# Two scale chunks of the first condition as column products, a freed bank for the first shift, a separate semaphore for one load, and wide products in the last norm

## The chip, the cores and the metric

The kernel runs on one core of a Trainium2 chip. The time is the device time of one execution in microseconds. Five engines work side by side: TensorE (PE; its weight loads are listed as PEld), VectorE (DVE), ScalarE (ACT), GpSimd (POOL) and SyncE (SP), which issues all the DMAs. They meet only at semaphores.

## The reference

Input `x` (256 tokens of 1024 features) and a context `ctx` of 256 tokens pass through two transformer layers with adaptive norms, then `x` alone through a hybrid layer and a last norm. What the change touches is the very first norm and the very last:

```python
def adaln(cond, w, b):
    m = jax.nn.silu(cond) @ w + b
    return m.reshape(m.shape[:-1] + (N_MOD, D_MODEL))

def modulated_norm(h, g, m, k):
    return rmsnorm(h, g) * (1.0 + m[..., k + 1, :]) + m[..., k, :]
...
m = adaln(c, ada_w[i], ada_b[i])[:, None]
mc = adaln(c_ctx, ada_w[i], ada_b[i])[None]
h = half_ffn(h, m, 0, g[0], g[1], ffn_w_in[i, 0], ffn_w_out[i, 0])
...
return rmsnorm_2(x, norm_final)
```

There are two conditions, `c` for the latents and `c_ctx` for the context. `m[k]` is called the shift and `m[k+1]` the scale. `ada_w` has 9 x 1024 columns for each of the two layers, and all are needed, but the first norm needs only the first 1024 (shift) and the next 1024 (scale) of layer 0.

## The kernel before

Activations are kept transposed: features on the 128 partitions, in 8 chunks `c` (`CH` is 8), and tokens along the free axis, 512 of them (context and latents) in the first two layers and 256 at the end. Every product with a weight is made as three fp32r products, `w_hi·u_hi`, `w_lo·u_hi`, `w_hi·u_lo` (lines 1555, 1556, 1559). ScalarE rounds each raw weight tile to `w_hi` (line 771), GpSimd subtracts to get `w_lo` (line 751), in a ring of six tiles. The activations are split alike into `u_hi` (ACT, line 837) and `u_lo` (DVE, line 1186). The order of work on each engine is the order in which the code is written.

**The opening.** The norm's total over features is one product with ones (line 1684); ACT makes `rstd` of it (lines 791 and 799), signalled as `first_rstd`. For each chunk `c`:

- The shift's 128 values for both conditions are made on TensorE by `shift(c)`: eight products of a 128x128 piece of `ada_shift[c]` with the 2-column `silu_t` (line 1693), into bank `SUMS + c % 2`. ACT adds the bias (line 854, tile `mcol`).
- The scale's 128 values are made on DVE by two dot products over 1024 elements, one for each condition (`dot`, line 1104, tile `ada_sum`, with `silu_c`, the silu of the condition spread over all partitions, line 843). `a_col` (line 1268) is `(scale + 1) * gain`.
- DVE then makes `v = h * a_col * rstd` for both token halves (line 1172), and between them `u_lo` of the chunk before (line 1186). ACT makes `u_hi` of `v` and the shift.
- TensorE multiplies chunk `k` of `u` with four weight tiles, twelve 512-column products, after it has made `shift(k + 1)`: for `k` of 2 and more the order on TensorE is `shift(k + 1)`, then the twelve products of chunk `k`. The last of each three waits for `u_lo` of its chunk.

After chunk 7, DVE starts the first feed-forward block: 18 steps `m`, in each of which it makes two more tiles of `ada_w` (four dots) and then the gate product of step `m` (lines 1321, 1324, 1326). TensorE may start step `m` when the gate of step `m - 3` is there.

**The end.** In the last feed-forward block, the residual is added chunk by chunk as TensorE finishes it (DVE, line 1336), ACT squares it (line 814) and DVE sums the squares (line 1167). Two products with ones and two ACT instructions give `rstd`, and DVE makes the output in eight products of 256 columns, `h * gain * rstd` (line 1538). SyncE stores it in three DMAs (line 738), chunks 0 to 2, 3 to 5, 6 and 7.

Of the kernel before, what the change touches and what calls it, by code (L numbers as in the profile page):

```python
# [28 lines left out]
RAW_ITEMS = 9  # L29
FULL_U = slice(0, 256)  # L30
# [12 lines left out]
ADA_FREE = 4  # L43
ADA_OUT = (3, 3, 3, 3, 2, 2)
# [309 lines left out]
def build(nc, A):  # L354
# [110 lines left out]
    scale_in, shift_in = [sem(f"scale_in{c}") for c in range(CH)], [sem(f"shift_in{c}") for c in range(CH)]  # L465
    first_sq, first_sum, first_rstd = sem("first_sq"), sem("first_sum"), sem("first_rstd")
# [12 lines left out]
    out_ready, out_done = sem("out_ready"), sem("out_done")  # L479
# [44 lines left out]
    def norm_gain(b, m, c):  # L524

        if m is None:
            g = COL["norm2"] + b["part"] * CH + c
            return col[:, g:g + 1]
        return a_col[:, 3 * m + b["part"], c:c + 1]

# [136 lines left out]
    def _(sp):  # L667
# [68 lines left out]
        for c0, c1 in ((0, 3), (3, 6), (6, CH)):  # L736
            sp.wait_ge(out_ready, c1)
            sp.dma_start(A["out"][:, c0:c1, :], final[:, c0:c1, :]).then_inc(out_done, 16)
# [24 lines left out]
    def _(act):  # L763
# [76 lines left out]
        def first_norm(b):  # L840
            heads_to(0)
            act.wait_ge(consts_in, 32)
# [8 lines left out]
            for c in range(CH):  # L851
                act.wait_ge(shift_sum, c + 1)
                bias = COL["ada_b"] + c
                scalar.activation(mcol[:, :, c:c + 1], psum[:, SUMS + c % 2, 0:2].rearrange("p (c o) -> p c o", o=1),
# [71 lines left out]
        def output(b):  # L926
# [23 lines left out]
            for i, (j, tok, _) in enumerate(pieces):  # L950
# [127 lines left out]
    def _(dve):  # L1078
# [15 lines left out]
        dve.wait_ge(consts_in, 32)  # L1094
# [161 lines left out]
        def first_norm(b):  # L1256
# [6 lines left out]
            for c in range(CH):  # L1263
                dve.wait_ge(scale_in[c], 16)
                for i in range(2):
                    dot(first_tile(c), i, 2 * c + i, 0, ada_sum[:, c % 2, i:i + 1], 0)
                dve.wait_ge(ada_dot, 2 * c + 2 + ADA0)
                vec.tensor_scalar(a_col[:, 0:6:3, c:c + 1], ada_sum[:, c % 2, :].rearrange("p (c o) -> p c o", o=1),
# [9 lines left out]
            for p, tok in enumerate(halves(FULL)):  # L1278
                u_low(b, p, tok, CH - 1)
            dve.sem_inc(m_done, ADA_FIRST)  # L1280
# [255 lines left out]
        for c in range(CH):  # L1536
            g = COL["norm2"] + 3 * CH + c
# [5 lines left out]
    def _(pe):  # L1543
# [136 lines left out]
        def start_phase(b, tiles):  # L1680
# [32 lines left out]
            for k in range(2, CH):  # L1713
                if k + 1 < CH:
                    shift(k + 1)
# [362 lines left out]
```

## Time and profile before

| | |
|---|---|
| median of 3 runs | 2410.27 us (2409.76 to 2411.99) |
| profiled execution, its own time | 2406.9 us |
| its span | 2405.0 us |
| PE busy | 2329.1 us (97%) |
| DVE busy | 1577.9 us (66%) |
| ACT busy | 910.3 us (38%) |
| POOL busy | 1354.8 us (56%) |
| opening, up to DVE's first dot of the feed-forward block | 61.66 us |
| granted clock, mean | 0.999 |

The span is the time from the first to the last recorded instruction or transfer; the execution's own time is 1.9 us longer. The profiled execution was 3.4 us shorter than the median of the timed ones. A row of the timeline gives the start, the duration, the engine, the line and the operation with the tile it writes and the ones it reads; in brackets stands how long the engine had been idle and what it had waited for. "x16" is a count of merged instructions. A plain fp32 product is recorded as two instructions, so the eight products of one shift are a row of x16.

### The profile page before, as it was taken

How to read it: one execution, taken by the hardware profiler on the slowest of the kernel's cores; microseconds unless marked ns; L12 is line 12 of the kernel's file. 1: busy time of each engine (PE TensorE's matmuls, PEld its weight loads, DVE VectorE, ACT ScalarE, POOL GpSimd, SP SyncE). 2: the span in 40 equal slices, each digit the busy share in tenths (PEclk: the TensorE clock that was granted, in tenths of full speed). 3: DMA queues.
4: the chain of work that ended last, by engine and by line, in shares of the span. 5: the costliest groups of instructions: out<-in, count | busy, mean ns of one | idle time of the engine just before them, and what ended most of it. 6: DMA issues, size and time to landing. Idle time of an engine off the chain costs nothing.

```text
span 2405.0 us, 36289 instructions
## 1 busy us (share of the span) xinstructions
PE 2329.1 (97%) x14528; PEld 2062.9 (86%) x14528; DVE 1577.9 (66%) x2518; ACT 910.3 (38%) x1466; POOL 1354.8 (56%) x700
## 2 busy tenths in 40 slices
PE   7999999999989999999999998899999999999998
PEld 5887789777688777898778897789999999999998
DVE  8999796666679997958983126567527614534661
ACT  4222224455442222233222235554444444545443
POOL 4555455222235554654554443278878887468886
PEclk9999999999999999999999999999999999999999
DMA  7655352211025553534533332145555564345554
GB/s 278 214 189 184 139 206 85 71 54 62 27 88 202 196 182 139 205 109 166 178 129 93 97 90 72 53 149 184 179 156 192 180 189 159 99 145 185 183 179 136
DMA packets 97510, 350.11 MB, mean 146 GB/s; under 512 B 10944, under 2 KB 10944, under 8 KB 96960
## 3 DMA queue, kind: packets, MB, share of 16 engines
q1 hardware_dynamic: 97344, 347.81, 43.2%
q8 instruction: 115, 1.88, 0.3%
q14 instruction: 51, 0.42, 0.1%
HBM read 346.71 MB, written 1.05 MB: 145 GB/s over the span
## 4 chain that ended last, share of the span: by engine, by line
PE 51%; DVE 13%; issue 4%; ACT 2%; POOL 1%; DMA 1%; DVEq 0%; ACTq 0%
PE psum L1555 16%; PE psum L1559 16%; PE psum L1556 16%; DVE psum L1104 7%; PE psum L1904 1%; DVE sq L1321 1%; POOL w_lo L751 1%; PE psum L1876 1%; ACT w_hi L771 1%; DVE gu_hi L1324 0%; DVE psum L1194 0%; DVE h L1200 0%; PE psum L1884 0%; DVE u_lo L1413 0%; DVE pcomb L1386 0%
## 5 line engine op out<-in xcount | busy, mean ns | idle before, releaser
L751 POOL TENSOR_TENSOR w_lo<-w_raw,w_hi 128x1024 fp32r<-128x1024 f32 (+3 forms) x696 | 1354.6, 1971 | 1033.4 <-ACT w_hi L771 1032.7
L1555 PE MATMUL psum<-u_hi,w_hi 128*128 128x256 f32 (+2 forms) x2912 | 975.4, 335 | 16.3 <-POOL w_lo L751 5.3
L1559 PE MATMUL psum<-u_lo,w_hi 128*128 128x256 f32 (+2 forms) x2912 | 947.8, 325 | 3.3 <-DVE u_lo L1186 2.0
L1556 PE MATMUL psum<-u_hi,w_lo 128*128 128x256 f32 (+2 forms) x2912 | 945.8, 325 | 0.0
L771 ACT ACTIVATE w_hi<-w_raw 128x1024 fp32r<-128x1024 f32 (+1 forms) x522 | 529.1, 1030 | 337.7 <-PE psum L1559 275.5
L1555 PEld LDWEIGHTS psum<-u_hi,w_hi 128*128 128x128 f32 x2912 | 553.1, 190 | 98.2 <-issue 25.7
L1559 PEld LDWEIGHTS psum<-u_lo,w_hi 128*128 128x128 f32 x2912 | 552.7, 190 | 52.8 <-DVE u_lo L1186 4.8
L1556 PEld LDWEIGHTS psum<-u_hi,w_lo 128*128 128x128 f32 x2912 | 553.4, 190 | 44.3 <-issue 3.4
L1555 PE MATMUL psum<-gu_hi,w_hi 128*128 128x256 f32 (+1 forms) x1188 | 379.2, 319 | 0.0
L1556 PE MATMUL psum<-gu_hi,w_lo 128*128 128x256 f32 (+1 forms) x1188 | 378.1, 318 | 0.0
L1559 PE MATMUL psum<-gu_lo,w_hi 128*128 128x256 f32 (+1 forms) x1188 | 378.1, 318 | 0.0
L1555 PEld LDWEIGHTS psum<-gu_hi,w_hi 128*128 128x128 f32 x1188 | 226.3, 190 | 15.8
L1556 PEld LDWEIGHTS psum<-gu_hi,w_lo 128*128 128x128 f32 x1188 | 226.3, 191 | 15.7
L1559 PEld LDWEIGHTS psum<-gu_lo,w_hi 128*128 128x128 f32 x1188 | 226.3, 190 | 15.3
L918 ACT ACTIVATE sq<-psum 128x512 f32<-128x512 f32 x66 | 39.5, 599 | 456.1 <-DVE gu_lo L1326 399.5
L1326 DVE TENSOR_TENSOR gu_lo<-sq,gu_hi 128x512 fp32r<-128x512 f32 (+1 forms) x132 | 184.3, 1396 | 4.5
L1104 DVE CUSTOM_DVE_ANT_0 psum<-ada_lo,silu_c 128x1024 f32<-128x1024 f32 x96 | 170.1, 1772 | 10.1 <-DMA ada_lo<-in_ada_w 8.5
L1210 DVE TENSOR_TENSOR rstd<-rstd,sq 128x256 f32<-128x256 f32 (+1 forms) x58 | 43.1, 743 | 192.0 <-ACT sq L867 99.6
L1104 DVE CUSTOM_DVE_ANT_0 psum<-ada_hi,silu_c 128x1024 f32<-128x1024 f32 x96 | 160.1, 1668 | 1.7
L1124 DVE TENSOR_SCALAR mcol<-ada_sum,col 128x2 f32<-128x2 f32 x128 | 151.0, 1180 | 4.5
L1321 DVE TENSOR_TENSOR sq<-sq,psum 128x512 f32<-128x512 f32 (+1 forms) x110 | 63.6, 578 | 78.6 <-PE psum L1559 71.6
L1324 DVE CAST gu_hi<-sq 128x512 fp32r<-128x512 f32 (+1 forms) x132 | 102.9, 780 | 4.6
(173 smaller groups left out, 2060.4 us busy)
## 6 DMA issues: line engine op xcount, KB each, us to landing
w_raw<-in_ffn_in SPq DMA_DIRECT2D x264, 512.0 KB, 3.7
w_raw<-in_ffn_out SPq DMA_DIRECT2D x96, 448.0 KB, 3.4
ada_hi<-in_ada_w SPq DMA_DIRECT2D x48, 512.0 KB, 3.6
ada_lo<-in_ada_w SPq DMA_DIRECT2D x48, 512.0 KB, 3.5
w_raw<-in_ffn_out SPq DMA_DIRECT2D x48, 512.0 KB, 3.6
ada_out<-in_ada_w SPq DMA_DIRECT2D x32, 512.0 KB, 4.4
w_raw<-in_b_qkv SPq DMA_DIRECT2D x30, 512.0 KB, 3.4
w_raw<-in_da_in SPq DMA_DIRECT2D x24, 512.0 KB, 3.5
```

Source lines behind the costliest of these rows:

```text
L751: last = pool.tensor_tensor(w_lo[:, slot, w], w_raw[:, slot, w], w_hi[:, slot, w].bitcast(F32), ALU.subtract)
L771: scalar.activation(w_hi[:, slot, 0:cols], w_raw[:, slot, 0:cols], ACT.Copy).then_inc(hi_ready, 1)
L918: scalar.activation(s_up[:, j, tok], psum[:, pair_bank(m), tok], ACT.Silu).then_inc(silu_ready, 1)
L1104: vec.tensor_tensor_reduce(out=psum[:, junk:junk + 2, :].rearrange("p a b -> p (a b)"), in0=tile, in1=silu_c[:, c, :], scale=1.0, scalar=0 ...
L1124: vec.tensor_scalar(mcol[:, :, n:n + 1], ada_sum[:, n % 2, :].rearrange("p (c o) -> p c o", o=1), col[:, bias:bias + 1], None, ALU.add).th ...
L1210: vec.tensor_tensor(sqsum[:, tok], sqsum[:, tok], sq[:, i % 2, tok], ALU.add).then_inc(yacc_ready, 1)
L1321: vec.tensor_tensor(s_up[:, j, tok], s_up[:, j, tok], psum[:, pair_bank(m) + 1, tok], ALU.mult)\
L1324: vec.tensor_copy(gu_hi[:, m, tok], s_up[:, j, tok]).then_inc(ghi_ready, 1)
L1326: vec.tensor_tensor(gu_lo[:, m, tok], s_up[:, j, tok], gu_hi[:, m, tok].bitcast(F32), ALU.subtract)\
L1555: mm(out, w_hi[:, slot, w], x_hi, start=start and n == 0, stop=False)
L1556: mm(out, w_lo[:, slot, w], x_hi, start=False, stop=False)
L1559: last = mm(out, w_hi[:, slot, w], x_lo, start=False, stop=stop and n == len(ks) - 1)
```

## The change

Four edits.

1. `SCALE_COLS = 2`: the scale of chunks 6 and 7 is no longer made by dots on DVE. Its weights come in the layout of the shift's (`ada_scale`), and TensorE makes it with eight 2-column products per chunk, in `scale(c)`, into bank 0 or 1. `scale(6)` stands after `shift(6)` and ahead of the products of chunk 5, `scale(7)` after `shift(7)` and ahead of the products of chunk 6. DVE waits for the sum (`scale_sum`) before it makes `a_col`.
2. The first shift goes into bank `RSTD` instead of `SUMS`, which holds the norm's total; so `shift(0)` no longer waits for `first_rstd`, and `shift(1)` does.
3. The load of `silu_c` has a semaphore of its own, so that its silu waits for that load and not for the table of columns too; ACT waits for the columns before it adds the first shift's bias.
4. In the last norm ACT makes `h * gain` of each chunk after its square, and DVE multiplies with `rstd` in three products of 768, 768 and 512 columns instead of eight of 256.

```diff
-        sp.dma_start(silu_c[:, :, :], A["cond"]).then_inc(consts_in, 16)
+        sp.dma_start(silu_c[:, :, :], A["cond"]).then_inc(silu_c_in, 16)
         for c in range(CH):
-            sp.dma_start(first_tile(c), A["ada_w"][CH + c]).then_inc(scale_in[c], 16)
+            by_cols = c >= CH - SCALE_COLS
+            scale = A["ada_scale"][c - CH + SCALE_COLS] if by_cols else A["ada_w"][CH + c]
+            sp.dma_start(first_tile(c), scale).then_inc(scale_in[c], 16)
...
-            act.wait_ge(consts_in, 32)
+            act.wait_ge(silu_c_in, 16)
             scalar.activation(silu_c[:, :, :], silu_c[:, :, :], ACT.Silu).then_inc(silu_c_ready, 1)
...
                 act.wait_ge(shift_sum, c + 1)
+                if c == 0:
+                    act.wait_ge(consts_in, 16)
...
                     square(nb, 0, LAT, j)
+                    if nb["n"] == len(BLOCKS):
+                        g = COL["norm2"] + 3 * CH + j
+                        scalar.activation(final[:, j, :], h[:, j, LAT], ACT.Copy, scale=col[:, g:g + 1]).then_inc(final_gain, 1)
...
             for c in range(CH):
-                dve.wait_ge(scale_in[c], 16)
-                for i in range(2):
-                    dot(first_tile(c), i, 2 * c + i, 0, ada_sum[:, c % 2, i:i + 1], 0)
-                dve.wait_ge(ada_dot, 2 * c + 2 + ADA0)
+                if c < CH - SCALE_COLS:
+                    dve.wait_ge(scale_in[c], 16)
+                    for i in range(2):
+                        dot(first_tile(c), i, 2 * c + i, 0, ada_sum[:, c % 2, i:i + 1], 0)
+                    dve.wait_ge(ada_dot, 2 * c + 2 + ADA0)
+                    total = ada_sum[:, c % 2, :]
+                else:
+                    dve.wait_ge(scale_sum, c - CH + SCALE_COLS + 1)
+                    total = psum[:, c % 2, 0:2]
...
-        for c in range(CH):
-            g = COL["norm2"] + 3 * CH + c
-            vec.scalar_tensor_tensor(out=final[:, c, :], in0=h[:, c, LAT], scalar=col[:, g:g + 1], in1=psum[:, RSTD, LAT],
-                                     op0=ALU.mult, op1=ALU.mult).then_inc(out_ready, 1)
+        for n, c in enumerate(FINAL_PARTS):
+            dve.wait_ge(final_gain, c.stop)
+            k = c.stop - c.start
+            vec.tensor_tensor(final[:, c, :], final[:, c, :], psum[:, RSTD:RSTD + 1, LAT].broadcast_to([128, k, SEQ]), ALU.mult)\
+               .then_inc(out_ready, 1)
...
             def shift(c):
                 pe.wait_ge(shift_in[c], 16)
-                if c == 0:
+                if c == 1:
                     pe.wait_ge(first_rstd, 1)
...
+            def scale(c):
+
+                pe.wait_ge(scale_in[c], 16)
+                if c == CH - SCALE_COLS:
+                    pe.wait_ge(ada_dot, 2 * c + ADA0)
+                for k in range(CH):
+                    last = mm(psum[:, c % 2, 0:2], first_tile(c)[:, k * 128:(k + 1) * 128], silu_t[:, k, :],
+                              start=k == 0, stop=k == CH - 1)
+                last.then_inc(scale_sum, 1)
...
                 if k + 1 < CH:
                     shift(k + 1)
+                if k >= CH - 1 - SCALE_COLS and k + 1 < CH:
+                    scale(k + 1)
                 for tile in tiles:
                     run(*tile, k)
```

TensorE in the opening, from the last products of chunk 4 on, before: `shift(6)` stands between them and the products of chunk 5 (`first_b` holds the shift's weights).

```order
L1559 MATMUL psum<-u_lo,w_hi 128x512 [waits ulo_ready]
L1693 MATMUL psum<-silu_t,first_b 128x2 [waits shift_ready,shift_in6]
L1693 MATMUL psum<-silu_t,first_b 128x2 x7
L1555 MATMUL psum<-u_hi,w_hi 128x512 [waits uhi_ready]
L1556 MATMUL psum<-u_hi,w_lo 128x512
L1559 MATMUL psum<-u_lo,w_hi 128x512 [waits ulo_ready]
```

The same place after the change; the row with `first_a` is `scale(6)`.

```order
L1580 MATMUL psum<-u_lo,w_hi 128x512 [waits ulo_ready]
L1714 MATMUL psum<-silu_t,first_b 128x2 [waits shift_ready,shift_in6]
L1714 MATMUL psum<-silu_t,first_b 128x2 x7
L1724 MATMUL psum<-silu_t,first_a 128x2 [waits ada_dot,scale_in6]
L1724 MATMUL psum<-silu_t,first_a 128x2 x7
L1576 MATMUL psum<-u_hi,w_hi 128x512 [waits uhi_ready]
L1577 MATMUL psum<-u_hi,w_lo 128x512
L1580 MATMUL psum<-u_lo,w_hi 128x512 [waits ulo_ready]
```

Eight more 2-column products stand ahead of chunk 5's, and in the same way ahead of chunk 6's; nothing else on TensorE has moved.

VectorE in the opening, chunk 6, before (`v_63` is the tile `v` of the text; ISA is a dot or the reading of its sum):

```order
L1104 ISA psum,ada_sum<-first_a,silu_c 128x1024 [waits ada_dot,scale_in6]
L1104 ISA ada_sum 128x1
L1104 ISA psum,ada_sum<-first_a,silu_c 128x1024 [waits ada_dot]
L1104 ISA ada_sum 128x1
L1268 TENSOR_SCALAR a_col<-ada_sum,stat,col 128x2 [waits ada_dot]
L1172 SCALAR_TENSOR_TENSOR v_63<-h,a_col,rstd 128x256 [waits scale_step]
L1186 SCALAR_TENSOR_TENSOR u_lo<-v_63,mcol,u_hi 128x256 [waits uhi_ready]
L1172 SCALAR_TENSOR_TENSOR v_63<-h,a_col,rstd 128x256
L1186 SCALAR_TENSOR_TENSOR u_lo<-v_63,mcol,u_hi 128x256 [waits uhi_ready]
```

The same chunk after:

```order
L1287 TENSOR_SCALAR a_col<-psum,stat,col 128x2 [waits scale_sum]
L1186 SCALAR_TENSOR_TENSOR v_63<-h,a_col,rstd 128x256 [waits scale_step]
L1200 SCALAR_TENSOR_TENSOR u_lo<-v_63,mcol,u_hi 128x256 [waits uhi_ready]
L1186 SCALAR_TENSOR_TENSOR v_63<-h,a_col,rstd 128x256
L1200 SCALAR_TENSOR_TENSOR u_lo<-v_63,mcol,u_hi 128x256 [waits uhi_ready]
```

The two dots are gone from chunk 6 and from chunk 7. The `u_lo` in these rows is that of the chunk before, so `u_lo` of chunk 5 still stands behind `a_col` of chunk 6, which now waits for TensorE.

VectorE at the end, before:

```order
L1336 SCALAR_TENSOR_TENSOR h<-psum,h 128x256 [waits tile_used]
L1167 TENSOR_TENSOR sq<-psum,sq 128x256 [waits hacc_ready,hsq_ready]
L1538 SCALAR_TENSOR_TENSOR final<-h,col,psum 128x256 [waits hsq_ready,hacc_ready,rstd_h_ready]
L1538 SCALAR_TENSOR_TENSOR final<-h,col,psum 128x256 x7
L1977 UNCONDITIONAL_BRANCH
```

And after:

```order
L1356 SCALAR_TENSOR_TENSOR h<-psum,h 128x256 [waits tile_used]
L1181 TENSOR_TENSOR sq<-psum,sq 128x256 [waits hacc_ready,hsq_ready]
L1559 TENSOR_TENSOR final<-final,psum 128x768 [waits hsq_ready,hacc_ready,final_gain,rstd_h_ready]
L1559 TENSOR_TENSOR final<-final,psum 128x768 [waits final_gain]
L1559 TENSOR_TENSOR final<-final,psum 128x512 [waits final_gain]
L2010 UNCONDITIONAL_BRANCH
```

Eight instructions have become three, and eight copies with a gain have been added on ScalarE, one behind each square.

## Rows read from the trace of the kernel before

**Rows 1.** The page: span, and shares of the last chain by engine.
```profile
span 2405.0 us, 36289 instructions
...
PE 51%; DVE 13%; issue 4%; ACT 2%; POOL 1%; DMA 1%; DVEq 0%; ACTq 0%
```
**Rows 2.** Windows: stretch, length, busy us (instructions) by engine, clock, DMA, GB/s.
```profile
50.80:55.32 4.52, 4.52 (x29) 3.96 (x28) 4.42 (x10) 0.91 (x3) 0.00 (x0) 1.00 0.00 0
...
61.60:264.40 202.80, 201.83 (x880) 164.22 (x879) 199.08 (x238) 46.66 (x56) 113.76 (x36) 1.00 0.54 189
```
**Rows 3.** Waits from 63 to 270 us: total us, times, longest.
```profile
PEld psum L1555 <- DVE sq L1321: 5.5, 9, 1.3
```
**Rows 4.** Timeline of DVE, chunks 5 to 7 and the first body dot.
```profile
50.28 0.48 DVE L1186 SCALAR_TENSOR_TENSOR u_lo<-v,mcol,u_hi 128x256 fp32r<-128x256 f32 x1
50.68 1.23 DVE L1104 CUSTOM_DVE_ANT_0 psum<-first_a,silu_c 128x1024 f32<-128x1024 f32 x1
...
53.33 0.29 DVE L1268 TENSOR_SCALAR a_col<-ada_sum,stat,col 128x2 f32<-128x2 f32 x1
...
54.84 0.48 DVE L1186 SCALAR_TENSOR_TENSOR u_lo<-v,mcol,u_hi 128x256 fp32r<-128x256 f32 x1
...
60.52 0.89 DVE L1186 SCALAR_TENSOR_TENSOR u_lo<-v,mcol,u_hi 128x256 fp32r<-128x256 f32 x2 [0.64 <-ACT u_hi L837]
...
61.66 1.23 DVE L1104 CUSTOM_DVE_ANT_0 psum<-ada_hi,silu_c 128x1024 f32<-128x1024 f32 x1
```
**Rows 5.** Timeline of PE, products of chunk 4, `shift(6)`, chunk 5, `shift(7)`.
```profile
50.82 0.50 PE L1559 MATMUL psum<-u_lo,w_hi 128*128 128x512 f32 x1
...
53.24 1.84 PE L1693 MATMUL psum<-silu_t,first_b 128*128 128x2 f32 x16
...
54.94 0.49 PE L1555 MATMUL psum<-u_hi,w_hi 128*128 128x512 f32 x1
...
57.80 1.84 PE L1693 MATMUL psum<-silu_t,first_b 128*128 128x2 f32 x16
```
**Rows 6.** Timeline of ACT: the bias of shift 6.
```profile
55.11 0.26 ACT L854 ACTIVATE mcol<-psum,col 128x2 f32<-128x2 f32 x1 [3.61 <-PE psum L1693]
```
**Rows 7.** Timeline of the opening's start: ACT, DVE, PE.
```profile
13.65 1.91 ACT L843 ACTIVATE silu_c<-silu_c 128x2048 f32<-128x2048 f32 x1 [1.40 <-DMA col<-in_columns]
...
15.69 1.23 DVE L1104 CUSTOM_DVE_ANT_0 psum<-first_a,silu_c 128x1024 f32<-128x1024 f32 x1 [0.51 <-ACT silu_c L843]
...
18.37 6.96 PE L1693 MATMUL psum<-silu_t,first_b 128*128 128x2 f32 x32 [2.85 <-ACT rstd L799]
...
27.10 0.80 PE L1559 MATMUL psum<-u_lo,w_hi 128*128 128x512 f32 x1 [0.70 <-DVE u_lo L1186]
```
**Rows 8.** Timeline of SP and DVE: a tile for the body's third ada step.
```profile
64.25 0.91 SPq L677 DMA_DIRECT2D ada_lo<-in_ada_w  x2
...
73.25 1.22 DVE L1104 CUSTOM_DVE_ANT_0 psum<-ada_lo,silu_c 128x1024 f32<-128x1024 f32 x1
```
**Rows 9.** Timeline of PE: 512-column products early and later, and a long wait.
```profile
28.54 0.63 PE L1559 MATMUL psum<-u_lo,w_hi 128*128 128x512 f32 x1
...
41.55 0.40 PE L1559 MATMUL psum<-u_lo,w_hi 128*128 128x512 f32 x1
...
427.03 1.22 PE L1589 MATMUL psum<-sq,ones 128*128 128x256 f32 x2 [2.65 <-DVE sq L1167]
```
**Rows 10.** Timeline of the end, and a 512-column DVE product on PSUM.
```profile
82.78 0.68 DVE L1321 TENSOR_TENSOR sq<-sq,psum 128x512 f32<-128x512 f32 x1
...
2396.01 0.41 DVE L1167 TENSOR_TENSOR sq<-psum,sq 128x256 f32<-128x256 f32 x1
...
2397.65 0.47 ACT L791 ACTIVATE rstd<-psum,small 128x256 f32<-128x256 f32 x1 [0.94 <-PE psum L1594]
...
2398.57 3.22 DVE L1538 SCALAR_TENSOR_TENSOR final<-h,col,psum 128x256 f32<-128x256 f32 x8 [2.15 <-ACT psum L799]
...
2399.86 2.29 SPq L738 DMA_DIRECT2D out<-final  x3
```

More of the change, by code:

```diff
@@ L29 @@
 RAW_ITEMS = 9
+FINAL_PARTS = (slice(0, 3), slice(3, 6), slice(6, CH))
 FULL_U = slice(0, 256)
@@ L43 @@
 ADA_FREE = 4
+SCALE_COLS = 2
 ADA_OUT = (3, 3, 3, 3, 2, 2)
@@ L529, in norm_gain, with shift_bank @@
         return a_col[:, 3 * m + b["part"], c:c + 1]
+    def shift_bank(c):
+        return (RSTD, SUMS)[c % 2]
     def gate_bank(j):
@@ L735, in _ @@
                 load_whole(A[b["kind"] + "_out"], b["t_out"], 0, CH)
-        for c0, c1 in ((0, 3), (3, 6), (6, CH)):
-            sp.wait_ge(out_ready, c1)
-            sp.dma_start(A["out"][:, c0:c1, :], final[:, c0:c1, :]).then_inc(out_done, 16)
+        for n, c in enumerate(FINAL_PARTS):
+            sp.wait_ge(out_ready, n + 1)
+            sp.dma_start(A["out"][:, c, :], final[:, c, :]).then_inc(out_done, 16)
         sp.wait_ge(out_done, 48)
@@ L1279, in first_norm @@
                 u_low(b, p, tok, CH - 1)
+            dve.sem_inc(ada_dot, 2 * SCALE_COLS)
             dve.sem_inc(m_done, ADA_FIRST)
@@ L1534, in _ @@
             transition(b, BLOCKS[b["n"] + 1] if b["n"] + 1 < len(BLOCKS) else END)
-        for c in range(CH):
-            g = COL["norm2"] + 3 * CH + c
-            vec.scalar_tensor_tensor(out=final[:, c, :], in0=h[:, c, LAT], scalar=col[:, g:g + 1], in1=psum[:, RSTD, LAT],
-                                     op0=ALU.mult, op1=ALU.mult).then_inc(out_ready, 1)
+        for n, c in enumerate(FINAL_PARTS):
+            dve.wait_ge(final_gain, c.stop)
+            k = c.stop - c.start
+            vec.tensor_tensor(final[:, c, :], final[:, c, :], psum[:, RSTD:RSTD + 1, LAT].broadcast_to([128, k, SEQ]), ALU.mult)\
+               .then_inc(out_ready, 1)
     @block.tensor
@@ L1692, in shift @@
                 for k in range(CH):
-                    last = mm(psum[:, SUMS + c % 2, 0:2], first_tile(CH + c)[:, k * 128:(k + 1) * 128], silu_t[:, k, :],
+                    last = mm(psum[:, shift_bank(c), 0:2], first_tile(CH + c)[:, k * 128:(k + 1) * 128], silu_t[:, k, :],
                               start=k == 0, stop=k == CH - 1)
                 last.then_inc(shift_sum, 1)
+            def scale(c):
[6 more added lines that the diff above has]
+                last.then_inc(scale_sum, 1)
             def run(t, bank, tok, k):
@@ L2048 @@
     X["ada_shift"] = I["ada_w"][0][:, 0:D].reshape(CH, 128, CH, 128).transpose(2, 1, 0, 3).reshape(CH, 128, D)
+    n = 2 * D - SCALE_COLS * 128
+    X["ada_scale"] = I["ada_w"][0][:, n:2 * D].reshape(CH, 128, SCALE_COLS, 128).transpose(2, 1, 0, 3).reshape(SCALE_COLS, 128, D)
     X["ada_w"] = I["ada_w"].reshape(2, D, MODS, 128).transpose(0, 2, 3, 1).reshape(2 * MODS, 128, D)
```

9 lines of the change are left out of this document (5 added, 4 removed).

## The prediction, made before the changed kernel was run

> **What bounds the kernel now.** I read the page first: the chain that ended last lies 51% on TensorE and 13% on VectorE [rows 1]. Then the windows, to see where VectorE's part lies. From 61.6 to 264.4 us, the steps of the first feed-forward block that also make `ada_w` tiles, VectorE is busy 199.08 of 202.80 us [rows 2], and the little that is missing lies between single instructions; TensorE waits there for VectorE's gate products, 9 times and 5.5 us in all counted on its weight loads [rows 3]. So that stretch ends when VectorE is through, and it starts when VectorE leaves the opening, at 61.66 us [rows 4]. After it TensorE is the bound up to the end of the kernel but for the last norm. Whatever moves VectorE's 61.66 us moves the end by as much, as long as TensorE can follow.
>
> Last I read the opening itself, instruction by instruction. From chunk 4 on, the two engines go in step. TensorE waits for `u_lo` of chunk 4, which VectorE ends at 50.76 us (50.28 + 0.48) [rows 4], and goes on at 50.82 [rows 5]. In the window from 50.80 to 55.32 both are full: TensorE 4.52 and VectorE 4.42 of 4.52 us [rows 2]. The same work of the next chunk starts 4.56 us later on TensorE (53.24 and 57.80), so a chunk costs each of them about 4.56 us, side by side [rows 5].
>
> **The change, part by part.** All times below are those of the profiled execution: 2406.9 us, 1.9 more than its span.
>
> *Scale 6 and 7 on TensorE.* VectorE loses two dots per chunk, 53.33 - 50.68 = 2.65 us each time [rows 4]. TensorE gains a second block of eight 2-column products, at 1.84 us as `shift(6)` and `shift(7)` show it; I take 1.85 [rows 5]. By busy time alone this looks like a good trade, 5.3 us off VectorE for 3.7 on TensorE. What decides is the order. `u_lo` of chunk 5 stands on VectorE behind `a_col` of chunk 6, which now waits for `scale(6)`, and `scale(6)` stands on TensorE behind `shift(6)`, which stands behind all of chunk 4's products. And chunk 5's last factor on TensorE is that `u_lo`. What ran side by side becomes a row:
>
> - `shift(6)` has its result at 55.11, where ScalarE takes it [rows 6]. `scale(6)` has its result 1.85 later, at 56.96.
> - VectorE has been idle since 50.76 and now makes `a_col`, `v`, `u_lo`, `v`, `u_lo`. From the start of `a_col` to the end of the last `u_lo` it took 54.84 + 0.48 - 53.33 = 1.99 us [rows 4]. So `u_lo` of chunk 5 is whole at 58.95 instead of 55.32: 3.63 us later.
> - TensorE has passed `scale(6)` and two products of chunk 5 by then and stands still for some 1.3 us. Everything behind moves by 3.63 us: `shift(7)` too. The same happens once more with `scale(7)`: `u_lo` of chunk 6 is 7.26 us later.
> - `u_lo` of chunk 7 used to wait 0.64 us for ScalarE [rows 4], because shift 7 came late; it is now long there. So VectorE leaves the opening 7.26 - 0.64 = 6.6 us later.
>
> The end of VectorE's work is what the body hangs on, so this is +6.6 us at 264 us too. TensorE itself leaves the opening up to 7.3 us later; with up to 5.5 us of waits in the body to give back [rows 3] it would be late by 1.8 to 5 alone, so VectorE stays the bound. SyncE's next loads wait for TensorE to free a tile; the pair for the third ada tile was issued at 64.25 and used at 73.25 [rows 8]. The issue moves by 7.3 and the use by 6.6, so of 9 us between them 8.3 are left for a load that is half a megabyte as before. No new wait there.
>
> Bounds of the term: if the small block costs nothing beside what VectorE does, only the 1.99 us in a row stay for each chunk and the wait is smaller; by the rows the least is TensorE's own extra work, 2 x 1.85 = +3.7, less the short waits it has now, at most 0.7 as at 27.10 [rows 7]: +3. At most the term is 2 x (1.85 + 1.99 + 0.3) = +8.3, with an exchange of signals dearer than now. I take +6.6.
>
> *The load of silu_c.* ScalarE sat idle 1.40 us until the table of columns had landed, and VectorE then idle 0.51 us for the silu [rows 7]. VectorE cannot gain more than its own 0.51, since the instruction ahead of its first dot needs the columns. It is the bound from there, so I take -0.5; bounds 0 and -0.5.
>
> *The first shift in a free bank.* TensorE waited 2.85 us for `rstd` and no longer does [rows 7]. But it then waited 0.70 us for `u_lo` of chunk 0 at 27.10, which VectorE makes after the dots of chunk 1. The shift is earlier and the wait longer by the same amount. I take 0; bounds -0.7 (if ScalarE's earlier conversions get GpSimd out of VectorE's way sooner) and +0.5 (if they fall on it at a worse time).
>
> *The last norm.* Eight products took 3.22 us, 0.40 each [rows 10]. A product of 256 columns that reads PSUM took 0.41, one of 512 took 0.68 us [rows 10]: 0.27 for 256 columns more, so 0.95 for 768. Three of them are 0.95 + 0.95 + 0.68 = 2.58, less some 0.08 of overlap at each joint, 2.45. The gain is 0.75. The last store still follows the last product. ScalarE's copy of the last chunk lies in the 0.94 us in which it waits for TensorE [rows 10], if it is as long as its neighbours, 0.4 to 0.5; the seven others lie between tiles, where ScalarE has idle time. Bounds: -1.2, if width costs less than the rows say, and +0.5, if the repeated read of one bank is slow. I take -0.7.
>
> *Sum.* +6.6 - 0.5 + 0 - 0.7 = +5.4 us: 2406.9 becomes 2412.3 in a profiled execution. The median of the timed runs was 3.4 us above this one, so beside the median 2410.27 it is 2415.7 us.
>
> **A rule against this change.** At 28.54 us a 512-column product takes 0.63 us, at 41.55 it takes 0.40 [rows 9]: the first is the lower level, 1.2 GHz, and the second 2.4, though the granted clock stands at 1.00 in the windows. The 6.96 us of 2-column products from 18.37 on [rows 7] did not bring the clock up. A wait of 2.65 us between products of ones did not bring it down [rows 9]. The change puts blocks of 3.7 us of 2-column products and a wait of 1.3 us in a row, twice, with only ten full products between them. The trace has nothing like it at the upper level. If the clock fell there, the second pair of blocks and the products of chunks 6 and 7 would run at the lower one: 1.85 x 2 more for the small blocks, and about 3 more on TensorE behind them, of which VectorE sees only the first part: +3.7 on the sum, up to +5. The Trainium skill, "TensorE: Matmul & The Clock Gate", section "HAM oscillation — how this bites in real kernels", says that TensorE is set back to half rate when it stands idle too long between bursts. By that rule such a chunk order is at risk; by the row with 2.65 us it is not yet.
>
> **The rivals.**
>
> - *The clock falls* (12%): as above, +5.4 + 3.7 = +9.1, 2419.4 us. For: small products did not raise it. Against: none of the long waits in this kernel brought it down.
> - *VectorE catches up in the body* (20%): its dots there meet GpSimd's subtractions differently when TensorE and VectorE are shifted, and TensorE's own path decides. Then +7.3 - 5.5 - 0.5 - 0.7 = +0.6 at the least and some +3 in the middle: 2413 us, within the resolution. Against it: VectorE has no wait in 203 us.
> - *The trade works* (8%): `scale(6)` is there when VectorE arrives at it at 50.8. Then VectorE saves 5.3 and leaves at -5.8, TensorE has +3.7 - 0.5 = +3.2, less up to 5.5 given back [rows 3]; the later of the two decides: -2.3 at best, with the last norm -3.0, 2407.3 us. It decides only if `scale(6)` is through before 50.8, and in the written order it cannot start before the products of chunk 4 are. This one ends faster than before.
> - *My mechanism* (60%): 2413.5 to 2418 us, with the terms' bounds.
>
> **How the numbers follow.** A measurement of this kernel can tell 0.2% from no change, 4.8 us here: slower means above 2415.1, faster below 2405.5. My mechanism is centred 0.6 above the line, so about 60% of its 60 lie above it, 38 in 100; the fallen clock gives 12 and the catching up 2: 52 in 100 slower. Faster needs the trade to work and more than its price, or a term I have not seen: 6. The rest, 42, is no change to be told. The range 2409 to 2420.5 leaves out the trade that works, and the dearest case of the clock.
>
> **What would show it.** In the changed profile: VectorE idle some 6 us between the `u_lo` of chunk 4 and `a_col` of chunk 6, released by the small products on TensorE (`first_a`), and again some 6 before chunk 7; TensorE waiting 1.3 to 2 us for `u_lo` after the first two products of chunks 5 and 6; the first body dot at about 67.8 us instead of 61.66; VectorE as full in the body as before, and step 18 of the body later by the same 6; first dot of all at 15.2; `final` in three rows, 2.5 us in all. It is wrong if VectorE's first body dot comes before 64 us, or if the body gives back more than 1 us of its delay, or if 512-column products behind the small blocks take 0.63 us.

## The result: 0.5% slower, and the profile after

| | before | after |
|---|---|---|
| median | 2410.33 us (2407.70 to 2411.99, 6 runs) | 2422.04 us (2416.01 to 2422.37, 6 runs) |
| ratio | | 1.0045, 95% interval [1.0034, 1.0056] |
| profiled execution, its own time | 2406.9 us | 2422.03 us |
| its span | 2405.0 us | 2420.2 us |
| first dot of the feed-forward block | 61.66 us | 71.24 us |
| ScalarE's first `u_hi` of the second block | 407.24 us | 418.04 us |

The forecast was +5.4 us, 2415.7 (2409 to 2420.5). The sign was the likelier one, but +11.7 us lies outside the range.

VectorE in the opening of the changed kernel, to be set beside [rows 4]:

```profile
49.73 0.48 DVE L1200 SCALAR_TENSOR_TENSOR u_lo<-v,mcol,u_hi 128x256 fp32r<-128x256 f32 x1
57.92 0.28 DVE L1287 TENSOR_SCALAR a_col<-psum,stat,col 128x2 f32<-128x2 f32 x1 [7.71 <-PE psum L1724]
...
68.21 0.28 DVE L1287 TENSOR_SCALAR a_col<-psum,stat,col 128x2 f32<-128x2 f32 x1 [8.30 <-PE psum L1724]
...
71.24 1.23 DVE L1118 CUSTOM_DVE_ANT_0 psum<-ada_hi,silu_c 128x1024 f32<-128x1024 f32 x1
...
78.01 0.69 DVE L1346 TENSOR_TENSOR gu_lo<-sq,gu_hi 128x512 fp32r<-128x512 f32 x1
82.44 2.89 DVE L1118 CUSTOM_DVE_ANT_0 psum<-ada_lo,silu_c 128x1024 f32<-128x1024 f32 x1 [3.74 <-DMA ada_lo<-in_ada_w]
```

The two waits of `a_col` for the column sums (L1724) are those that were forecast, but 7.71 and 8.30 us long. At 82.44 stands one that was not: VectorE waits 3.74 us for a tile of `ada_w`.

TensorE at the same place, to be set beside [rows 5]; L1714 is the shift, L1724 the scale, and the row at 65.42 is `scale(7)`, whose weights lie in a tile named `first_b`:

```profile
45.71 0.69 PE L1580 MATMUL psum<-u_lo,w_hi 128*128 128x512 f32 x1 [0.79 <-DVE u_lo L1200]
46.20 0.63 PE L1576 MATMUL psum<-u_hi,w_hi 128*128 128x512 f32 x1
...
54.25 1.84 PE L1714 MATMUL psum<-silu_t,first_b 128*128 128x2 f32 x16
55.95 1.93 PE L1724 MATMUL psum<-silu_t,first_a 128*128 128x2 f32 x16
...
59.96 0.79 PE L1580 MATMUL psum<-u_lo,w_hi 128*128 128x512 f32 x1 [1.50 <-DVE u_lo L1200]
60.55 0.63 PE L1576 MATMUL psum<-u_hi,w_hi 128*128 128x512 f32 x1
...
65.42 2.74 PE L1724 MATMUL psum<-silu_t,first_b 128*128 128x2 f32 x16
68.03 0.77 PE L1576 MATMUL psum<-u_hi,w_hi 128*128 128x512 f32 x1
68.60 0.63 PE L1577 MATMUL psum<-u_hi,w_lo 128*128 128x512 f32 x1
70.25 0.80 PE L1580 MATMUL psum<-u_lo,w_hi 128*128 128x512 f32 x1 [1.02 <-DVE u_lo L1200]
```

A 512-column product is recorded with 0.39 us at the upper level (2.4 GHz) and 0.63 at the lower (1.2 GHz); the records of neighbours overlap, so that the next one starts 0.23 or 0.43 us later. The level fell three times: at 45.7, behind a shift and a wait of 0.79; at 60, behind `shift(6)`, `scale(6)` and a wait of 1.50; and in `scale(7)`, which takes 2.74 us where `scale(6)` took 1.93. The first of the three stands ahead of every product that the change adds. Windows of the same stretch (columns as in [rows 2]) show it as granted clock:

```profile
45.00:50.00 5.00, 4.29 (x14) 3.47 (x14) 4.89 (x10) 0.57 (x2) 0.37 (x1) 0.66 0.00 0
...
50.21:60.00 9.79, 8.29 (x59) 7.32 (x59) 1.95 (x5) 2.40 (x6) 0.00 (x0) 0.97 0.00 0
60.00:75.00 15.00, 13.98 (x59) 11.60 (x60) 6.65 (x15) 2.75 (x6) 0.00 (x0) 0.68 0.00 1
75.00:87.00 12.00, 12.00 (x55) 9.93 (x54) 8.05 (x13) 4.85 (x6) 5.66 (x3) 1.00 0.91 347
```

The loads of the body: SyncE issues `ada_lo` behind the last products of chunk 7, at 75.92 where it was 64.25 [rows 8], and they share the DMA engines with all the others (0.91 in the window above).

```profile
74.86 1.01 SPq L689 DMA_DIRECT2D w_raw<-in_ffn_in  x2
75.92 0.91 SPq L684 DMA_DIRECT2D ada_lo<-in_ada_w  x2
```

The opening's first rows, beside [rows 7], and the tail, beside [rows 10]:

```profile
12.68 1.91 ACT L852 ACTIVATE silu_c<-silu_c 128x2048 f32<-128x2048 f32 x1 [0.64 <-DMA silu_c<-in_cond]
...
14.99 1.23 DVE L1118 CUSTOM_DVE_ANT_0 psum<-first_a,silu_c 128x1024 f32<-128x1024 f32 x1
...
16.01 3.58 PE L1714 MATMUL psum<-silu_t,first_b 128*128 128x2 f32 x16 [0.69 <-DMA first_b<-in_ada_shift]
...
26.39 0.80 PE L1580 MATMUL psum<-u_lo,w_hi 128*128 128x512 f32 x1 [1.91 <-DVE u_lo L1200]
...
2412.33 0.49 ACT L974 ACTIVATE final<-h,col 128x256 f32<-128x256 f32 x1
...
2414.30 2.42 DVE L1559 TENSOR_TENSOR final<-final,psum 128x768 f32<-128x768 f32 x3 [2.15 <-ACT psum L808]
```

VectorE's first dot is 0.70 us earlier, the first shift no longer waits for `rstd` (its wait has gone to `u_lo`, 1.91 instead of 0.70), and the three wide products take 2.42 us instead of 3.22. In these rows the small edits do what they were meant to.

### The profile page after: what moved, and what is told of

Same layout as the page of the kernel before. It is cut to its first block, busy times and chain, and to the rows that moved or that the text cites. A ratio compares the mean times of both kernels' runs of the same rounds, so it can differ in the third digit from the quotient of the medians.

```text
span 2420.2 us, 36350 instructions
## 1 busy us (share of the span) xinstructions
PE 2342.9 (97%) x14560; PEld 2075.7 (86%) x14560; DVE 1567.3 (65%) x2505; ACT 913.7 (38%) x1474; POOL 1354.1 (56%) x700
## 4 chain that ended last, share of the span: by engine, by line
PE 44%; DVE 7%; issue 2%; ACT 2%; DMA 0%; POOL 0%; DVEq 0%; ACTq 0%
PE psum L1576 14%; PE psum L1580 14%; PE psum L1577 14%; DVE psum L1118 3%; PE psum L1937 1%; PE psum L1909 1%; ACT w_hi L780 1%; PE psum L1917 0%; POOL w_lo L760 0%; DVE u_lo L1433 0%; DVE sq L1341 0%; DVE pcomb L1406 0%; DVE stat L1491 0%; DVE psum L1208 0%; DMA w_raw<-in_ga_in 0%
```

## The experiments

Eleven kernels ran, each timed against the kernel before on the same chip. "First dot" is VectorE's first of the feed-forward block, "second block" ScalarE's first `u_hi` there, both in the profiled execution; the clock is the mean granted clock of all the runs, beside that of the kernel before on the same chip. Microseconds beside before are the ratio times 2410; the kernel before took 2411.50, 2410.45 and 2410.87 us in the median on the chips of the experiments, so two kernels are better compared by their ratios than by their medians.

Theory A, when the first runs were made: the order makes a row (TensorE's small products, VectorE's wait, TensorE's wait), and that is the price. B: the early first shift disturbs the clock's rise. C: TensorE's extra small products and their clock are the price.

| kernel | median us | ratio, 95% | first dot | second block | clock (before) |
|---|---|---|---|---|---|
| before | 2410.33 | | 61.66 | 407.24 | |
| after | 2422.04 | 1.0045 [1.0034, 1.0056] | 71.24 | 418.04 | 0.9938 |
| e1, small edits alone | 2409.53 | 0.9996 [0.9988, 1.0005] | 61.27 | 406.74 | 0.9963 (0.9962) |
| e10, same, early loads | 2410.50 | 0.9993 [0.9985, 1.0002] | 61.30 | 406.90 | 0.9965 (0.9963) |
| e9, wide products unused | 2413.76 | 1.0010 [1.0001, 1.0018] | 64.57 | 410.79 | 0.9962 (0.9963) |
| e11, 2-column ones apart | 2415.19 | 1.0020 [1.0011, 1.0029] | 64.53 | 410.58 | 0.9958 (0.9963) |
| e6, 2-column ones in a row | 2417.99 | 1.0028 [1.0019, 1.0037] | 66.78 | 414.54 | 0.9948 (0.9968) |
| e2, scale columns alone | 2425.55 | 1.0058 [1.0045, 1.0070] | 73.41 | 420.56 | 0.9922 (0.9962) |
| e4, scale between products | 2416.35 | 1.0020 [1.0009, 1.0031] | 64.28 | 409.96 | 0.9958 (0.9962) |
| e5, `u_lo` ahead of the wait | 2418.03 | 1.0028 [1.0018, 1.0037] | 65.41 | 410.46 | 0.9945 (0.9962) |
| e3, ones behind the scale | 2422.20 | 1.0045 [1.0033, 1.0057] | 69.59 | 418.39 | 0.9956 (0.9968) |
| e7, early loads in after | 2421.76 | 1.0044 [1.0032, 1.0056] | 71.42 | 416.99 | 0.9932 (0.9968) |
| e8, small products first | 2418.96 | 1.0031 [1.0019, 1.0043] | 64.28 | 412.98 | 0.9932 (0.9968) |

**e1: the small edits alone.** No scale by columns, everything else of the change.

```diff
-SCALE_COLS = 2
+SCALE_COLS = 0
```

> All 8 scale chunks are made by dots on VectorE again; the first shift's bank, the silu's own load and the wide last norm stay. Theory A (the scale products on TensorE carry the whole loss): the loss of 11.7 us is gone and the rest gains 0.5 in the opening and 0.8 in the last norm: -1.3 us against before, the first body dot at 61.0 to 61.2 us instead of 61.66 and 71.24. Theory B (the early first shift lets TensorE's clock rise and fall at worse times): some of the loss stays, +1 to +4 us, and windows of the opening show a granted clock under 1.00.

0.9996, -1.0 us with an interval from -2.9 to +1.2; the first dot 0.39 earlier. The early first shift does no harm that could be seen in the times. The loss is in the scale columns.

Theory B did expect a fall of the clock in the opening, and one stands in four profiles, from 45 to 50 us (granted clock 0.66 in each): those of the changed kernel, e3, e7 and e9. TensorE's code is the same up to there in e1, e10, e5, e6 and e11, and their profiles show 1.00. The same window in e1:

```profile
45.00:50.00 5.00, 5.00 (x33) 4.47 (x33) 4.89 (x9) 1.23 (x4) 2.20 (x2) 1.00 0.00 1
```

In the four, the 512-column products first reach the upper level at 34.9 to 35.7 us, in the five others at 37.1 to 38.2. So this fall comes and goes between executions of the same code and is not made by the scale columns; in the changed kernel's profile it costs about 1 us (`shift(6)` starts at 54.25, in e1 at 52.85, before at 53.24). Whether the early first shift makes it more frequent is not settled: the kernel before and e2, which lack it, show no such fall, but they are two profiles.

**e2: the scale columns alone.** The other three edits undone.

```diff
-        return (RSTD, SUMS)[c % 2]
+        return (SUMS, RSTD)[c % 2]
...
-        sp.dma_start(silu_c[:, :, :], A["cond"]).then_inc(silu_c_in, 16)
+        sp.dma_start(silu_c[:, :, :], A["cond"]).then_inc(consts_in, 16)
```

> Only the scale of chunks 6 and 7 on TensorE; the first shift, the silu's load and the last norm are as before. Theory A: the whole loss and none of the small gains: +11.7 + 1.3 = +13 us, first body dot near 71.8 us. Theory B (the early first shift has a part in it): less, +8 to +10 us, with no fall of the clock ahead of the first scale product.

1.0058, +14 us. Theory A's number holds (the first dot is at 73.41, where it has 71.8), but its reason only in part: the granted clock from 66 to 76 us is 0.52, and `shift(7)` and `scale(7)` take twice their time. (A window, and TensorE's rows of those products.)

```profile
66.00:76.00 10.00, 8.98 (x32) 7.56 (x32) 5.52 (x13) 2.56 (x4) 0.00 (x0) 0.52 0.00 0
```
```profile
63.52 3.41 PE L1708 MATMUL psum<-silu_t,first_b 128*128 128x2 f32 x16
66.78 3.55 PE L1718 MATMUL psum<-silu_t,first_b 128*128 128x2 f32 x16
```

**e4: the scale in the middle of the products of chunks 3 and 4**, in the bank that the shift leaves free, so that the sums come early.

```diff
-                if k >= CH - 1 - SCALE_COLS and k + 1 < CH:
-                    scale(k + 1)
-                for tile in tiles:
+                for tile in tiles[:2]:
+                    run(*tile, k)
+                if k in (3, 4):
+                    scale(k + 3)
+                for tile in tiles[2:]:
                     run(*tile, k)
```

> The same scale products on TensorE, but scale(6) stands in the middle of chunk 3's products and scale(7) in the middle of chunk 4's, in the bank that the shifts have free, and VectorE makes a_col of them at once, a chunk early. Same work on every engine as after. Theory A (the order makes the loss: VectorE's u_lo stands behind a_col, and a_col behind two blocks of small products): the two exchanges of 3.6 us each and the falls of the clock go, and only TensorE's extra 3.7 us less its short waits stay: first body dot near 65 us, +2 to +3.5 us against before. Theory C (the extra work on TensorE is the loss, wherever it stands): +10 us or more as now.

The opening is as A has it: first dot 64.28, clock 1.00 from 50 to 76 in the profile. The time, +4.8 us, is more than its +2 to +3.5; the runs go from 2411.57 (clock 0.997) to 2424.55 (0.992). VectorE still waits 4.34 us for the sum of `scale(7)`, at 54.58, and then in another place, for `u_hi`, since `shift(7)` comes later by the scale's time:

```profile
63.13 0.89 DVE L1200 SCALAR_TENSOR_TENSOR u_lo<-v,mcol,u_hi 128x256 fp32r<-128x256 f32 x2 [3.29 <-ACT u_hi L846]
```

TensorE is busy without a gap from 50 to 76 us here as it is in the kernel before. It had nothing to spare for the work that it was given. The profiled execution took 2412.99 us and is one of the three fastest of the eleven; what the clock does in the slower ones no profile shows.

**e5: the order of the change, but VectorE makes `u_lo` of the chunk before ahead of its wait.**

```diff
                 else:
+                    for p, tok in enumerate(halves(FULL)):
+                        u_low(b, p, tok, c - 1)
                     dve.wait_ge(scale_sum, c - CH + SCALE_COLS + 1)
```

> As after, but for chunks 6 and 7 VectorE makes u_lo of the chunk before ahead of its wait for the scale's sum. TensorE's order is as in after. Theory A: TensorE no longer waits for u_lo behind the scale products; each chunk costs TensorE its extra block of 1.85 us and no more, VectorE leaves the opening after scale(7) by two v and two u_lo: first body dot at 65 to 67 us instead of 71.24, +5 to +7 us against before. The clock then should fall less, since no wait follows the small products. Theory C (the small products themselves make the clock fall): the falls stay, first body dot at 68 or later, +8 us or more.

First dot 65.41, time +6.7 us: A's. TensorE no longer waits in the row `shift`, `scale`, `u_lo`. It is 4.0 us under the changed kernel; that is the price of VectorE's order, with what clock it costs. The intervals of the two touch. The profile, with a granted clock of 1.00 from 50 to 76 us, is that of the fastest of its eleven runs (2413.32); their mean clock is 0.9945, under the kernel before's 0.9962, so in others the clock does fall, and no profile shows where.

**e6: TensorE's extra products, and nobody who uses them.** VectorE makes all its dots as before; the sums of the 2-column products are not used. One wait for them is left, behind VectorE's last `u_lo`: 0.44 us in the profile of e6, 0.28 in e9 and 1.54 in e11, which have it too.

```diff
-            dve.sem_inc(ada_dot, 2 * SCALE_COLS)
+            dve.wait_ge(scale_sum, 2)
...
+                if k in (5, 6):
+                    scale(k + 1)
                 for tile in tiles:
                     run(*tile, k)
```

> The order of the kernel before on VectorE (all sixteen dots; first shift in the free bank, own semaphore, wide last norm kept), plus the eight 2-column products of scale(6) and scale(7) on TensorE, whose sums nobody reads. This is TensorE's extra work alone, without VectorE waiting for it. Theory A (VectorE's wait is the price): first body dot at 61 to 63.5, only as far as shift(7) is late; TensorE's 3.7 us more are partly given back by its 5.5 us of waits in the body; time +0.5 to +3 beside 2409.5. Rival C (the extra TensorE work and its clock are the price): time +7 or more, 2416 to 2420, with slow products behind the small ones.

1.0028, +6.7 us: the rival C, not A. TensorE is never idle from 50 to 66 us, and its clock falls all the same, in the second block of small products (its rows, and the window):

```profile
52.89 1.84 PE L1714 MATMUL psum<-silu_t,first_b 128*128 128x2 f32 x16
54.59 2.84 PE L1723 MATMUL psum<-silu_t,first_a 128*128 128x2 f32 x16
57.87 0.63 PE L1577 MATMUL psum<-u_hi,w_lo 128*128 128x512 f32 x1
```
```profile
50.00:66.00 16.00, 16.00 (x90) 14.37 (x89) 9.51 (x20) 4.01 (x10) 0.00 (x0) 0.77 0.00 1
```

One of the twelve runs took 2409.45 us at a mean clock of 0.998; the eleven others had 0.993 to 0.996 and took 2414 to 2421. The profile of e7 (below) shows the same once more, `scale(6)` at the lower level right behind `shift(6)`, with TensorE busy without a gap from 50 to 58 us:

```profile
55.37 2.67 PE L1724 MATMUL psum<-silu_t,first_a 128*128 128x2 f32 x16
```

**e9: the same, with wide products.** Eight products of ones, 128 columns, in place of each eight of 2 columns: 2.03 us a block, a little longer than 1.93.

```diff
-                for k in range(CH):
-                    last = mm(psum[:, shift_bank(c - 1), 0:2], first_tile(c)[:, k * 128:(k + 1) * 128], silu_t[:, k, :],
-                              start=k == 0, stop=k == CH - 1)
+                for k in range(WIDE):
+                    last = mm(psum[:, shift_bank(c - 1), 0:128], ones[:, :], ones[:, :], start=True, stop=True)
```

> The kernel with the unused 2-column products (e6, 2418.0 us), with eight 128-column products of ones in place of each eight 2-column ones. They take TensorE as long (1.95 us for eight) and use no more of the result. Theory D (a row of 3.7 us of 2-column products brings the granted clock down although TensorE is never idle): no fall from 50 to 76 us, first body dot at 61 to 63.5 instead of 66.78, time 2409 to 2413. Rival E (it is TensorE's added time, whatever the products): as e6, first body dot at 65 to 67, 2416 to 2420.

The clock stands at 1.00 in the same window:

```profile
50.00:66.00 16.00, 16.00 (x111) 14.67 (x111) 11.61 (x26) 4.80 (x10) 0.00 (x0) 1.00 0.00 1
```

First dot 64.57 and +2.4 us (the interval from +0.2 to +4.3), 4.3 us under e6 by the ratios; the intervals do not touch. The mean clock of its runs is that of the kernel before (0.9962 and 0.9963), e6's is lower (0.9948 and 0.9968). The median, 2413.76, is just above the 2413 of theory D, and the first dot is outside its 61 to 63.5. So of e6's loss about 4 us go with the kind of product and its clock, and not with TensorE's time. The rest is the time: `shift(7)` comes later, and `u_hi` and `u_lo` behind it.

The profile of e9 holds the fall from 45 to 50 us, and `shift(6)` starts in it at 54.04, 1.2 us behind e1's; of the first dot's 3.3 us beside e1 these are 1.2. Such an early fall does not by itself keep the clock up afterwards: e7 has it too, and its clock falls again in `scale(6)`. At the first dot e6 is 2.21 us behind e9 and at the second block 3.75; between the two VectorE waits for a tile `ada_lo`, 4.32 us in e6 and 3.21 in e9.

**e11: the unused 2-column products apart from the shift's**, in the middle of the chunk.

```diff
-                if k in (5, 6):
-                    scale(k + 1)
-                for tile in tiles:
+                for tile in tiles[:2]:
+                    run(*tile, k)
+                if k in (5, 6):
+                    scale(k + 1)
+                for tile in tiles[2:]:
                     run(*tile, k)
```

> The kernel with the unused 2-column products (e6), with these in the middle of the chunk's products and not right behind the shift's: the same number, in rows of 1.85 and 1.93 us with six full products between them. Theory D1 (the length of a row of small products decides): the clock stays up in most runs, time 2410 to 2414. Rival D2 (their share of the chunk decides, wherever they stand): the clock falls in most runs as in e6, time 2415 to 2420.

+4.8 us, between e9 and e6, and the interval touches both; runs from 2410.57 (clock 0.998) to 2422.81 (0.993). Apart they are not safe; whether they are better than in a row isn't shown, since the intervals of e11 and e6 overlap. Whether D1 or D2 is the better rule stays open.

**e3: ones behind each scale**, ten products of 128 columns, to fill TensorE's wait.

```diff
                     scale(k + 1)
+                    for _ in range(10):
+                        mm(psum[:, k % 2, 128:256], ones[:, :], ones[:, :], start=True, stop=True)
```

> The changed kernel with ten products of ones (128 columns) behind scale(6) and behind scale(7), while TensorE would stand waiting for u_lo. They add no arithmetic to the result. Theory A+clock (the row on TensorE costs what was forecast, and the granted clock that falls at 46 to 49, 60 to 63 and 66 to 73 us costs the rest of the opening): the clock stays at 1.00 from 50 to 76 us, the wait for u_lo before the products of chunk 5 shrinks from 1.50 us to near nothing, and VectorE's first body dot comes at 67.5 to 69 instead of 71.24; the time is 2 to 5 us under the changed kernel's, 2417 to 2420. Rival (the opening is longer by the order alone, the slower clock is only seen): first body dot at 71 to 72, time 2421 to 2423.

The clock stayed at 1.00 from 50 to 66 us and the first dot came at 69.59, but the ones took 2.48 us, more than the wait that they were to fill, and at 66.37 they ran at the lower level themselves (4.09 us). The first dot came 1.65 us earlier than in the changed kernel, but the load of `ada_lo` behind TensorE's products only 0.96 (74.96); VectorE waited 4.88 us for it, the second block starts no earlier (418.39), and the time is the same. It settles nothing on the price of the clock; e9 does.

**e7: the changed kernel with the loads of `ada_lo` at 28 us** beside those of `ada_hi`; their memory is free from the start.

```diff
-                    for x in range(2):
+                    for x in {0: range(4), 1: ()}.get(k, range(2)) if b["n"] == 0 else range(2):
                         load_ada("body", first + 2 * k + x, (2 * k + x) % ADA_SLOTS)
```

> The changed kernel, with the loads of the tiles for the body's second ada step (ada_lo, two of 512 KB) issued with those of the first step at about 28 us instead of behind the products of chunk 7. If the 3.74 us wait of VectorE for ada_lo at 82.4 us costs time: it goes to 0, the conversion to gu_hi that was short (0.43 us) becomes longer again, and the time falls by 0.5 to 2.5 us, 2419.5 to 2421.5. If it was only a wait in place of a slower conversion: the same as the changed kernel within 0.5, 2421.5 to 2422.5.

The wait is gone, and the second block starts at 416.99, 9.75 behind the kernel before, as its first dot does (9.76). In the changed kernel the first dot is 9.58 behind and the second block 10.80. So the wait of 3.74 us cost 1.1 us: most of it stood in place of slower conversions (`gu_hi` took 0.43 us without GpSimd beside it, 2.56 before). The median, 2421.76, can't show so little beside 2422.04.

**e8: the small products ahead of the wide ones.** `scale(6)` in the middle of chunk 3, `scale(7)` ahead of chunk 4, `shift(6)` and `shift(7)` in its middle, with the early loads; VectorE was to find all its sums there.

```diff
+                if k == 4:
+                    scale(7)
                 for tile in tiles[:2]:
                     run(*tile, k)
+                if k == 3:
+                    scale(6)
+                if k == 4:
+                    shift(6)
+                    shift(7)
```

> The same work as the changed kernel in another order: scale(6) in the middle of chunk 3's products, scale(7) ahead of chunk 4's, shift(6) and shift(7) in the middle of chunk 4's, in banks of their own, and the early loads of ada_lo. VectorE then needs nothing late from TensorE. Theory A (the order is the price, the trade itself is even): VectorE's first body dot at 58.5 to 61 instead of 61.27 without scale columns; TensorE, which is 3.7 us later at the end of the opening, gives the pace of the body's first steps; time 2407.5 to 2410.5. Rival (both engines are full, moving work gives nothing and the small products cost clock): 2411 to 2415.

+7.5 us. The two shifts took 6.82 us instead of 3.7, the clock from 50 to 66 was 0.60, and VectorE waited 2.64 us for the sum of `scale(7)`, 4.21 and 2.14 for `u_hi`, and 2.89 for the first gate's products.

```profile
55.44 6.82 PE L1723 MATMUL psum<-silu_t,first_b 128*128 128x2 f32 x32
```
```profile
50.00:66.00 16.00, 16.00 (x75) 14.65 (x75) 6.90 (x18) 4.80 (x10) 0.00 (x0) 0.60 0.01 1
```

This order was to spare VectorE its waits and made the rows of small products longer, and the clock fell in them. e4 keeps them apart and pays with TensorE's time. I found no order in which the trade pays.

**e10: the small edits alone with the early loads.**

> The three small edits without the scale columns (first shift in the free bank, silu on its own load, wide last norm), and the loads of ada_lo early. If the small edits are worth what their rows say, -0.5 and -0.8 us beside before, and the early loads nothing where VectorE does not wait for them: ratio 0.9990 to 0.9998, 2409 to 2410. If the earlier first shift disturbs the clock's rise: 2411 to 2414.

0.9993, from -3.6 to +0.5 us. With e1 that is twice about a microsecond under the kernel before, as the rows of the opening and the tail say (-0.5 and -0.8), and twice inside what the measurement can't tell from nothing. It is the best version of these, but not shown to beat the kernel before.

## Why the prediction was wrong, by its steps

*The ladder.* By the ratios, times 2410: small edits alone -1.0 and -1.7; with TensorE's extra time in wide products +2.4; the same time in 2-column products +6.7; with VectorE waiting for the sums +10.8. So some 4 us each for TensorE's time, for the clock that the kind of product costs, and for the waits with their clock. Neighbouring steps differ by little more than their intervals, and those of e6 and the changed kernel touch; the whole is far outside them.

*The order, +6.6 us: right in size.* VectorE's first dot is 9.58 us late, where the forecast had 6.1. The difference is the clock, read from the rows: the products of chunk 4 ended at 54.25 instead of 53.24 (+1.0), six products from 59.96 to 62.69 took 2.73 instead of 1.37 (+1.4), and `scale(7)` 2.74 instead of 1.93 (+0.8): 3.2 together, and 6.1 + 3.2 = 9.3. The first of these, 1.0, is the fall that stands ahead of the added products; it is chance of this execution and no cost of the order. The size is thus worked out from rows; no run has this order with the clock up throughout. And the reasoning was too narrow in one place. It took VectorE's waits for the whole price and put the bound from TensorE's own work at +3. e9 shows that bound to be about right (+2.4), and the two other orders that were tried, e4 and e8, did not get under it.

*The clock, 12%: the step that failed.* The sum has no term for the clock, on the ground that the waits and blocks of the change would not bring it down. The rival had the mechanism and nearly the size, +3.7, and the prediction's own sign of being wrong came: 512-column products behind the small blocks take 0.63 us (60.55). What failed is the weighing, "none of the long waits in this kernel brought it down". That was read wrongly from [rows 9]: the product behind the wait of 2.65 us lasts 1.22 us, and the ones behind it ran slowly too. Here they are, with the window in which the granted clock is 0.60, and then the same place in e1, where the wait was 1.79:

```profile
427.03 1.22 PE L1589 MATMUL psum<-sq,ones 128*128 128x256 f32 x2 [2.65 <-DVE sq L1167]
428.04 2.98 PE L1602 MATMUL psum<-ones 128*128 128x128 f32 x16
```
```profile
427.00:431.00 4.00, 3.97 (x20) 3.79 (x21) 1.61 (x4) 1.77 (x4) 0.00 (x0) 0.60 0.00 0
```
```profile
425.82 0.70 PE L1609 MATMUL psum<-sq,ones 128*128 128x256 f32 x2 [1.79 <-DVE sq L1181]
426.36 1.95 PE L1622 MATMUL psum<-ones 128*128 128x128 f32 x16
```

So the clock did fall there in the kernel before. And the stronger sign, that 6.96 us of 2-column products had not raised it [rows 7], was noted and then given no weight. The page "TensorE: Matmul & The Clock Gate" of the Trainium skill, section "HAM oscillation — how this bites in real kernels", puts the risk in idle time between bursts. Two of the three falls here do stand behind idle time, though of only 0.79 and 1.50 us, and the one in the kernel before, at 427 us, behind 2.65; e6 goes beyond it: no idle time, and a fall.

*A load that was said to be hidden, 0: wrong by +1.1.* [Rows 8] were read as 8.3 us left for the load. The issue moved by 11.7 and the first dot by 9.6, so 6.9 of the 9.0 us were left, and the load took 6.5 (75.92 to 82.44). But VectorE came to it at 78.70, 4.1 us sooner than its delay alone puts it, since its conversions were short without GpSimd beside them. Most of that lead would have been lost again, as e7 shows: only 1.1 of the 3.74 us of the wait was a cost.

*VectorE full in the body, so nothing is given back: right.* The delay of the first dot is there at the second block, to 0.1 us in e7.

*The silu's load, the first shift, the last norm (-0.5, 0, -0.7): right.* VectorE's first dot -0.70; the first shift's gain went into the wait for `u_lo`, 1.91 instead of 0.70; the last products -0.80.

*The rest.* From the second block to the last norm the profiled execution loses another 4.9 us beside the one of before. TensorE ran at the lower level at 725, 1476, 1493 and 1803 us, where that one did not. That is not the change's doing in the main: the profile of e1, without scale columns and at 2409.22 us, has four such places too, from 648, 712, 1464 and 1480 us on, and loses 3.3 us in the same stretch (1994.6 us, where the kernel before took 1991.3 and the changed one 1996.3). They differ from run to run, in the kernel before too, whose 27 runs beside e1 took 2407.35 us at a mean clock of 0.998 to 2413.46 at 0.995; its profiled one was 3.4 us under its median and has none of the four. The 1.6 us that are left beside e1 are not explained. By the profiles, then, first dot, load and last norm come to 9.6 + 1.2 - 0.8 = +10.0 us, beside +10.8 by the ratio and +11.7 by the medians, and forecast were +5.4.

*A slip in the chances.* 60% of 60 is 36 and not 38, so slower had 50 in 100. Nothing hangs on it.

*The rivals.* "VectorE catches up" and "the trade works" (20% and 8%) are refuted for this kernel: nothing was given back by the second block, and e4, e5 and e8, with earlier sums or `u_lo` ahead of the wait, bring no gain over the kernel before.

## What to carry to other kernels

Before work is moved from one engine to another, add up both engines' time in that stretch: here both were full, TensorE's share 4.52 of 4.52 us a chunk and VectorE's 4.42, and freeing VectorE of 2.65 us a chunk brought no gain in any order. In e4, where the clock stayed up, TensorE came later by its 1.84 us for each block, and VectorE waited for it. Price a block of very narrow products twice, by its time and by what TensorE's granted clock does behind it; the second was as much as the first. And a late row has a late load behind it: a transfer that waits for one engine's progress is hidden only as long as its consumer is delayed by as much. Last, before a wait is called harmless for the clock, look at how long the products behind it take, and not only at the wait.

## What the runs showed of the hardware

- TensorE's clock can fall while the engine is never idle. With 1.84 and 1.93 us of 2-column fp32 products back to back it fell within the second block (2.84 us instead of 1.93) in the profile of e6; with 128-column ones of 2.03 us in their place it did not (e9), and the two kernels are 4.3 us apart by their ratios. In e7 it fell in the same block (2.67 us).
- Nor is it certain: one of the twelve runs of e6 shows a mean clock of 0.998 and 2409.45 us, and the profile of e5, with the same blocks back to back, shows 1.00 from 50 to 76 us.
- The clock's course differs between executions of the same code: in nine profiles with the same work on TensorE up to 45 us, it first rose at 34.9 to 35.7 us in four and at 37.1 to 38.2 in five, and only the four fell again between 45 and 50 us.
- A product of ones, 128 columns in fp32, takes 0.25 us at the upper level (ten in 2.48).
- A VectorE product of 768 columns with one operand read again from PSUM goes by its width: 768, 768 and 512 columns in 2.42 us, where eight of 256 took 3.22.
